# Recurrent scan of a 1024-wide block: mask tiles kept over both halves, first decays ahead of the clears, one product group moved behind another

## The chip, the cores and the metric

The kernel runs on one core of a Trainium2 chip. The metric is the device time of one execution in microseconds (us). The core has TensorE (PE: matmuls into PSUM), VectorE (DVE), ScalarE (ACT), GpSimd (POOL) and SyncE (SP), which here only issues DMAs. Each engine works through its own instructions in order and waits for the others on semaphores.

## The reference

The program is two transformer-like blocks over 512 latent and 256 context tokens, all in float32. The change touches one piece of the second block, the two-way recurrence of its even layer:

```python
def step(state, inp):
    r_t, w_t, k_t, v_t, kk_t, a_t = inp
    sa = jnp.einsum('bhvk,bhk->bhv', state, -kk_t)
    state = (state * w_t[:, :, None, :] + sa[..., None] * (kk_t * a_t)[:, :, None, :]
             + v_t[..., None] * k_t[:, :, None, :])
    return state, jnp.einsum('bhvk,bhk->bhv', state, r_t)
```

It runs forward and backward over 768 tokens, for eight heads of 64 features.

## The kernel before

The eight heads are done in two halves of four. `recurrence` runs three stages for each half: `prepare_stage` (decays, normalised keys, bonus terms), `scan_stage` (the recurrence) and `head_norm_stage`. A stage is a block of the five engines with a meeting point of all engines at its end, so nothing of a scan is issued before its preparation is over.

**The scan.** The 768 tokens are cut into 12 chunks of 64. Inside a chunk the recurrence is turned into matrix products. A 64x64 triangular inverse G is built in six levels: each level is a product group `x`, a turning `t`, a copy of both by ScalarE (`copy_xt`), a second product group `g_x`, and a masked copy into G by VectorE (`extend`). The groups of 16 small matmuls (64x64) that go with it on TensorE are:

- `a(c)`: decayed a by decayed b; `main_products(c, d)`: b and k by a and r; `b_k_turned(c)` and `v_turned(c)`: turnings;
- `z_from_chunk(c)` (L3056): the part of z that needs only the chunk (four waits: v copied, its factor masked, the state and y of the chunk before done); `z_from_state(c)`: the part that needs the state, added on top in PSUM;
- `u(c)`, `y_from_state(c)`, `s_products(c)`, `y_from_chunk(c)`: what follows from z.

Three chunks are under way at once. The order is written out by hand: a loop over q from -3 to 11 issues, on each engine, the steps of chunk q (its end), `now` = q+1 (levels 4 and 5), `new` = q+2 (levels 1 to 3) and `coming` = q+3 (its decays and first products). One turn of that loop is called a period below. Each engine's part is a list in program order, and an instruction that waits holds up all behind it on its engine.

**The start of a scan.** SP loads four constant mask tiles (`mask_before`, `masks_by_feature`, `unit_squares`, and `level_masks` as float32 into the area that the `residual` buffer lends) and, in the first half, the next keys. VectorE waits for all four, casts the level masks to 8 bits (L2935), and only then starts on the decays of chunk 0 (`decayed_a` L2868, `decayed_r` L2876). ScalarE computes the decay factors of chunk 0 (L2801), then waits for the cast before it goes on (`start_inverse` L2806, factors of chunk 1). TensorE waits for the masks and for two clears. GpSimd clears the state `S[0]` and `y` (L2775), then decays b and k of each chunk (L2784) and gathers v (L2788).

In the profile the buffers lent by `resid` are named `residual.1`, those lent by `gate_rows` (G, Z, masked a-b products, state) `gate_rows.1`, and PSUM `banks`.

Of the kernel before, what the change touches and what calls it, by code (L numbers as in the profile page):

```python
# [28 lines left out]
U8 = mybir.dt.uint8  # L29
# [332 lines left out]
def build(nc, dram, out_dram, debug=None):  # L362
# [12 lines left out]
    def sb(name, shape, dt=F32):  # L375
        return nc.alloc_sbuf_tensor(unique(name), shape, dt)

    def sem(name):
        return nc.alloc_semaphore(unique(name))
# [2116 lines left out]
    def recurrence(rcols, lora, r, k, v, mixT):  # L2496
        flat, flat2 = flat_of(resid), flat_of(gate_rows)
        with stage():
            kk = sb("kk", [P, 2, TOK])
            iclr, kdir = sb("iclr_then_b", [P, 4, TOK]), sb("k_dir", [P, 4, TOK])  # L2500
            run = sb("running_decay", [P, 4, NCH * CW])
            gam = sb("chunk_decay", [P, 2, 4, NCH])
            y = sb("y", [P, 2, TOK])
            for half in range(2):
                prepare_stage(half, rcols, lora, r, k, v, kk, iclr, kdir, run, gam, mixT, flat)
                if half == 0:
                    dump("kk", kk[:]); dump("kdir", kdir[:]); dump("run", run[:]); dump("bb", iclr[:]); dump("bv", mixT[:, 0:2, :])
                scan_stage(r, y, v, kk, iclr, kdir, run, gam, flat, flat2, k if half == 0 else None)
                head_norm_stage(half, rcols, lora, r, y, v, mixT, flat)
# [16 lines left out]

    def prepare_stage(half, rcols, lora, r, k, v, kk, iclr, kdir, run, gam, mixT, flat):

# [6 lines left out]
        with stage():  # L2535
# [10 lines left out]
            tots = sem("totals")  # L2546
            gam_made = sem("chunk_decays")
            with nc.Block() as block:
                @block.sync
                def _(sp):  # L2550
                    sp.dma_start(w2[:], dram["w2"][half]).then_inc(loaded, 16)
                    sp.dma_start(a2[:], dram["a2"][half]).then_inc(loaded, 16)
                    sp.dma_start(reset[:], dram["reset"].partition_broadcast(P)).then_inc(loaded, 16)

                @block.gpsimd
# [66 lines left out]
                def _(dve):  # L2622
# [18 lines left out]
                    dve.wait_ge(loaded, 48)  # L2641
                    scan(0)
                    scan(1)
                    finish_kdir(0)
# [29 lines left out]

    def scan_stage(r, y, v, kk, bb, kdir, run, gam, flat, flat2, k_next):


        with stage():
# [3 lines left out]
            def area(base, at, n=2):  # L2682
                return base[:, at * 256:(at + n) * 256]
# [30 lines left out]
            e = sb("decay_factors", [P, 2, 3, 4, CH])  # L2714
            before = sb("mask_before", [P, 2, CH])
            mask_H = sb("masks_by_feature", [P, 2, 4, CH])
            unit = sb("unit_squares", [P, CH])
            level = sb("level_masks", [P, LEVELS, 2, CH], U8)
            level_f32 = area(flat, 16, 3)
            loaded, zeroed, levels_cast, k_loaded = sem("loaded"), sem("zeroed"), sem("levels_cast"), sem("keys_loaded")  # L2720
            e_made, a_made, rc_made, bk_decayed = sem("factors_made"), sem("a_decayed"), sem("r_decayed"), sem("b_k_decayed")
# [40 lines left out]
            with nc.Block() as block:  # L2762
                @block.sync
                def _(sp):
                    for dst, src in ((before[:], dram["mask_before"]), (mask_H[:], dram["masks_by_feature"][:, 0:2]), (unit[:], dram["unit_squares"])):
                        sp.dma_start(dst, src).then_inc(loaded, 16)
                    sp.dma_start(level_f32, dram["level_masks"]).then_inc(loaded, 16)
                    if k_next is not None:
                        sp.dma_start(flat_of(k_next), parked_rkv[:, 2 * TOK:4 * TOK]).then_inc(k_loaded, 16)
                        sp.wait_ge(k_loaded, 16)  # L2770

                @block.gpsimd
                def _(pool):
                    for x in (S[0], y[:]):
                        nc.gpsimd.memset(x, 0.0).then_inc(zeroed, 1)  # L2775
                    for c in range(NCH):
                        if c >= 2:
                            pool.wait_ge(bkt_made, c - 1)
                        for src, places in ((bb, slice(1, 3)), (kdir, slice(0, 4, 3))):
                            for d in range(2):  # L2780
                                js = slice(2 * d, 2 * d + 2)
                                to = bk_flat[c % 2][:, d * 4 * CH:(d + 1) * 4 * CH].rearrange("p (a n) -> p a n", a=4)[:, places, :]
                                pool.wait_ge(e_made, 6 * c + 3 * d + 3)
                                nc.gpsimd.tensor_tensor(to, src[:, js, tokens(d, c)], e[:, c % 2, 2, js, :], ALU.mult).then_inc(bk_decayed, 1)  # L2784
                        if c >= 1:
                            pool.wait_ge(v_made, c)
                        for d in range(2):
                            nc.gpsimd.tensor_copy(v_now[:, d], v[:, :, tokens(d, c)]).then_inc(v_gathered, 1)  # L2788

                @block.scalar  # L2790
                def _(act):
# [40 lines left out]
                    for d in range(2):  # L2832
                        factors(0, d)
                    act.wait_ge(loaded, 64)
                    act.wait_ge(levels_cast, 1)
                    for q in range(-3, NCH):
# [24 lines left out]
                def _(dve):  # L2861
# [54 lines left out]

                    def new_state(c):
                        dve.wait_ge(s_made, c + 1)
                        nc.vector.tensor_tensor(S[(c + 1) % 2], S[c % 2], by_slot(s_out), ALU.add).then_inc(s_summed, 1)
# [5 lines left out]

                    def add_y(c):
                        dve.wait_ge(y2_made, c + 1)
                        for d in range(2):
# [4 lines left out]

                    dve.wait_ge(loaded, 64)
                    nc.vector.tensor_copy(level[:].rearrange("p l d n -> p (l d n)"), level_f32).then_inc(levels_cast, 1)  # L2935
                    dve.wait_ge(zeroed, 2)
                    dve.wait_ge(levels_cast, 1)
                    for q in range(-3, NCH):
# [32 lines left out]
                def _(pe):  # L2971
# [88 lines left out]
                    def z_from_state(c):  # L3060
                        if c >= 1:
                            pe.wait_ge(s_done, 2 * c)
# [41 lines left out]

                    pe.wait_ge(loaded, 64)
                    pe.wait_ge(zeroed, 2)
                    for q in range(-3, NCH):
# [31 lines left out]
                        if has_now:  # L3139
                            z_from_chunk(now)  # L3140
                            g_x(now, 5)
                        if has_new:
                            g_x(new, 2)
                        if coming < NCH:
                            a(coming)
# [325 lines left out]
```

## Time and profile before

| | |
|---|---|
| median of 3 runs | 3545.79 us (3544.70 to 3545.88) |
| profiled execution, own time | 3539.18 us |
| its span in the profile | 3537.4 us |
| mean granted TensorE clock | 0.948 of full |
| TensorE busy | 3202.2 us, 91% of the span |
| first scan, second scan | about 1683 to 1831 us, 1892 to 2040 us of the span |

Busy time of a matmul in the trace is pipelined and its end is modelled, so starts are read rather than ends. Line numbers (L2981) are those of the kernel before. A row of the timeline merges neighbouring instructions of one line; "x16" is their number and the length in front of the engine's name runs from the first one's start to the last one's end.

### The profile page before, as it was taken

To read this page: it belongs to the slowest core of one execution; us is meant where nothing else is said; L and a number is where in the kernel's file an instruction comes from. 1 tells how busy PE (TensorE), PEld (TensorE's weight loads), DVE (VectorE), ACT (ScalarE), POOL (GpSimd) and SP (SyncE) were. 2 spreads that over 40 slices of the span, in tenths; PEclk is the share of its full clock that TensorE was granted. 3 is DMA by queue.
4 is the path that set the end of the run, shared out by engine and by line. 5 is a ranking of instruction groups with operands and counts; after the bars stand their busy time and mean duration, and the time that the engine had idled before them with its cause. 6 is when DMAs were issued, how large, how long until landed. Compare 5 with 4: busy or idle time off the path is not lost. (4 is left out here: it accounts for less than half of the span.)

```text
span 3537.4 us, 53773 instructions
## 1 busy us (share of the span) xinstructions
PE 3202.2 (91%) x21886; PEld 2573.6 (73%) x21886; DVE 2208.1 (62%) x3940; ACT 1298.0 (37%) x2245; POOL 146.5 (4%) x222
## 2 busy tenths in 40 slices
PE   6989999997899969987887989998999998889999
PEld 5768877655788758865665867887887876678777
DVE  7678866696788675667555637554666336653344
ACT  2343333324433333245534534222233335642243
POOL 0300000200000000000211100000000000000000
PEclk9989999999999989998898989999999999999999
DMA  7424553112233422120000022333232121022221
GB/s 303 168 101 179 190 179 113 61 36 66 97 140 135 143 102 85 60 89 12 20 33 11 4 85 108 119 119 108 107 143 107 54 98 59 1 78 96 81 104 60
DMA packets 64773, 340.78 MB, mean 96 GB/s; under 512 B 15120, under 2 KB 16656, under 8 KB 29072
## 3 DMA queue, kind: packets, MB, share of 16 engines
q1 hardware_dynamic: 61616, 325.51, 26.2%
q0 software_dynamic: 2048, 9.48, 0.8%
q8 instruction: 174, 2.85, 0.3%
q10 hardware_dynamic: 864, 2.36, 0.2%
q14 instruction: 71, 0.58, 0.1%
HBM read 326.53 MB, written 10.79 MB: 95 GB/s over the span
## 5 line engine op out<-in xcount | busy, mean ns | idle before, releaser
L265 DVE TENSOR_TENSOR weight_lo<-weight_ring,weight_hi 128x1024 fp32r<-128x1024 f32 x341 | 423.1, 1242 | 170.2 <-ACT weight_hi L250 165.1
L250 ACT CAST weight_hi<-weight_ring 128x1024 fp32r<-128x1024 f32 x341 | 356.0, 1044 | 158.0 <-PE banks L422 91.9
L420 PE MATMUL banks<-hT_hi.1,weight_hi 128*128 128x512 f32 x896 | 365.7, 408 | 25.5 <-PEq L383 23.5
L421 PE MATMUL banks<-hT_lo.1,weight_hi 128*128 128x512 f32 x896 | 358.8, 400 | 0.0
L422 PE MATMUL banks<-hT_hi.1,weight_lo 128*128 128x512 f32 x896 | 358.5, 400 | 0.0
L420 PEld LDWEIGHTS banks<-hT_hi.1,weight_hi 128*128 128x128 f32 x896 | 171.4, 191 | 68.7 <-issue 26.4
L422 PEld LDWEIGHTS banks<-hT_hi.1,weight_lo 128*128 128x128 f32 x896 | 171.1, 191 | 41.9
L421 PEld LDWEIGHTS banks<-hT_lo.1,weight_hi 128*128 128x128 f32 x896 | 171.3, 191 | 41.5 <-issue 1.9
L420 PE MATMUL banks<-hT_hi.3,weight_hi 128*128 128x512 f32 (+1 forms) x512 | 174.6, 341 | 0.0
L422 PE MATMUL banks<-hT_hi.3,weight_lo 128*128 128x512 f32 (+1 forms) x512 | 173.3, 338 | 0.0
L421 PE MATMUL banks<-hT_lo.3,weight_hi 128*128 128x512 f32 (+1 forms) x512 | 173.1, 338 | 0.0
L319 DVE SCALAR_TENSOR_TENSOR side_sum<-weight_ring,silu_c2.1,side_sum 128x256 f32<-128x256 f32 x336 | 160.4, 477 | 0.1
L319 DVE SCALAR_TENSOR_TENSOR weight_ring<-weight_ring,silu_c2.1 128x256 f32<-128x256 f32 x336 | 160.3, 477 | 0.0
L531 PE MATMUL banks<-weight_hi,left_hi.6 128*128 128x512 f32 x360 | 145.8, 405 | 9.3 <-DVE weight_lo L265 9.3
L534 PE MATMUL banks<-weight_lo,left_hi.6 128*128 128x512 f32 x360 | 142.8, 397 | 0.0
L533 PE MATMUL banks<-weight_hi,left_lo.6 128*128 128x512 f32 x360 | 142.1, 395 | 0.0
L319 DVE SCALAR_TENSOR_TENSOR weight_ring<-weight_ring,silu_c1.1 128x256 f32<-128x256 f32 x280 | 135.6, 484 | 10.5
L420 PE MATMUL banks<-hT_hi.2,weight_hi 128*128 128x256 f32 (+1 forms) x336 | 115.1, 343 | 2.7 <-PEq L383 2.7
L421 PE MATMUL banks<-hT_lo.2,weight_hi 128*128 128x256 f32 (+1 forms) x336 | 114.1, 340 | 0.0
L422 PE MATMUL banks<-hT_hi.2,weight_lo 128*128 128x256 f32 (+1 forms) x336 | 114.0, 339 | 0.0
L422 PEld LDWEIGHTS banks<-hT_hi.3,weight_lo 128*128 128x128 f32 x512 | 96.4, 188 | 11.6
L421 PEld LDWEIGHTS banks<-hT_lo.3,weight_hi 128*128 128x128 f32 x512 | 96.6, 189 | 11.0
(746 smaller groups left out, 7324.1 us busy)
## 6 DMA issues: line engine op xcount, KB each, us to landing
weight_ring<-ff SPq DMA_DIRECT2D x64, 1024.0 KB, 5.0
weight_ring<-ada SPq DMA_DIRECT2D x48, 1024.0 KB, 4.8
weight_ring<-up SPq DMA_DIRECT2D x44, 1024.0 KB, 6.9
weight_ring<-ada_ffn SPq DMA_DIRECT2D x24, 1024.0 KB, 4.9
weight_ring<-down SPq DMA_DIRECT2D x20, 1024.0 KB, 4.9
weight_ring<-ada_mix SPq DMA_DIRECT2D x16, 1024.0 KB, 4.8
first_blocks.1<-ada_mix SPq DMA_DIRECT2D x8, 1024.0 KB, 11.9
weight_ring<-cv_in SPq DMA_DIRECT2D x8, 1024.0 KB, 4.8
```

What stands on the lines that cost most here:

```text
L250: self.nc.scalar.copy(hi, raw).then_inc(self.hi_made, 1)
L265: self.nc.vector.tensor_tensor(lo, raw, hi.bitcast(F32), ALU.subtract).then_inc(self.lo_made, 1)
L319: ins = self.nc.vector.scalar_tensor_tensor(out=to, in0=w[:, k, :], scalar=vec[:, k, v:v + 1], in1=to, op0=ALU.mult, op1=ALU.add)
L420: nc.tensor.matmul(out, w_hi, x_hi, start=first, stop=False)
L421: nc.tensor.matmul(out, w_hi, x_lo, start=False, stop=False)
L422: return nc.tensor.matmul(out, w_lo, x_hi, start=False, stop=last)
L531: one = nc.tensor.matmul(out, xh, hi[:, kk, :], start=(k == 0), stop=False)
L533: nc.tensor.matmul(out, xl, hi[:, kk, :], start=False, stop=False)
L534: last = nc.tensor.matmul(out, xh, lo[:, kk, :], start=False, stop=(k == k_tiles - 1))
```

## The change

Four edits:

1. The four mask tiles are allocated once for both halves. `prepare_stage` of half 0 loads them behind its own three loads on SP's queue, and VectorE casts the level masks between its first two scans over tokens. The scans load no masks and wait for none.
2. On GpSimd, the first chunk's decays of b and k come ahead of the clear of the state, and the clear of `y` comes behind the second chunk's.
3. The waits for the two clears move to the first instructions that need them.
4. On TensorE, `z_from_chunk(now)` moves from ahead of `g_x(now, 5)` to behind `g_x(new, 2)`.

```diff
+            masks = (sb("mask_before", [P, 2, CH]), sb("masks_by_feature", [P, 2, 4, CH]), sb("unit_squares", [P, CH]),
+                     sb("level_masks", [P, LEVELS, 2, CH], U8))
 ...
+            masks_loaded, levels_cast = sem("masks_loaded"), sem("levels_cast")
+            level_f32 = flat[:, 16 * 4 * CH:16 * 4 * CH + LEVELS * 2 * CH]
 ...
                     sp.dma_start(reset[:], dram["reset"].partition_broadcast(P)).then_inc(loaded, 16)
+                    if masks is not None:
+                        before, by_feature, unit, _ = masks
+                        sp.dma_start(level_f32, dram["level_masks"]).then_inc(masks_loaded, 16)
+                        sp.dma_start(before[:], dram["mask_before"]).then_inc(masks_loaded, 16)
+                        sp.dma_start(by_feature[:], dram["masks_by_feature"][:, 0:2]).then_inc(masks_loaded, 16)
+                        sp.dma_start(unit[:], dram["unit_squares"]).then_inc(masks_loaded, 16)
+                        sp.wait_ge(masks_loaded, 64)
 ...
                     scan(0)
+                    if masks is not None:
+                        dve.wait_ge(masks_loaded, 64)
+                        nc.vector.tensor_copy(masks[3][:].rearrange("p l d n -> p (l d n)"), level_f32).then_inc(levels_cast, 1)
                     scan(1)
 ... (scan_stage, SP)
-                    for dst, src in ((before[:], dram["mask_before"]), (mask_H[:], dram["masks_by_feature"][:, 0:2]), (unit[:], dram["unit_squares"])):
-                        sp.dma_start(dst, src).then_inc(loaded, 16)
-                    sp.dma_start(level_f32, dram["level_masks"]).then_inc(loaded, 16)
 ... (scan_stage, GpSimd)
-                    for x in (S[0], y[:]):
-                        nc.gpsimd.memset(x, 0.0).then_inc(zeroed, 1)
-                    for c in range(NCH):
+                    decay_bk(0)
+                    nc.gpsimd.memset(S[0], 0.0).then_inc(zeroed, 1)
+                    gather_v(0)
+                    decay_bk(1)
+                    nc.gpsimd.memset(y[:], 0.0).then_inc(zeroed, 1)
+                    gather_v(1)
+                    for c in range(2, NCH):
+                        decay_bk(c)
+                        gather_v(c)
 ... (scan_stage, ScalarE)
-                    act.wait_ge(loaded, 64)
-                    act.wait_ge(levels_cast, 1)
 ... (scan_stage, VectorE; new_state(0) now waits for zeroed 1, add_y(0) for zeroed 2)
-                    dve.wait_ge(loaded, 64)
-                    nc.vector.tensor_copy(level[:].rearrange("p l d n -> p (l d n)"), level_f32).then_inc(levels_cast, 1)
-                    dve.wait_ge(zeroed, 2)
-                    dve.wait_ge(levels_cast, 1)
 ... (scan_stage, TensorE; z_from_state(0) now waits for zeroed 1)
-                    pe.wait_ge(loaded, 64)
-                    pe.wait_ge(zeroed, 2)
 ...
                         if has_now:
-                            z_from_chunk(now)
                             g_x(now, 5)
                         if has_new:
                             g_x(new, 2)
+                        if has_now:
+                            z_from_chunk(now)
                         if coming < NCH:
                             a(coming)
```

## Rows read from the trace of the kernel before

**Rows 1.** The page's first line.

```profile
span 3537.4 us, 53773 instructions
```

**Rows 2.** Stretches: length, busy time by engine, clock granted, DMA share, GB/s.

```profile
1683.00:1689.70 6.70, 0.00 (x0) 0.00 (x0) 1.26 (x5) 2.02 (x9) 3.75 (x8) 0.50 0.65 201
...
1700.00:1702.00 2.00, 1.86 (x50) 1.44 (x44) 0.96 (x3) 1.49 (x5) 1.35 (x5) 0.89 0.00 0
...
1720.80:1731.50 10.70, 10.28 (x304) 8.81 (x304) 7.03 (x21) 6.09 (x18) 2.24 (x6) 1.00 0.02 5
1908.00:1909.00 1.00, 0.99 (x33) 0.80 (x32) 0.17 (x1) 0.95 (x3) 0.81 (x3) 0.68 0.00 0
```

**Rows 3.** Timeline, start of both scans: start, length, instruction, idle before and releaser.

```profile
1683.26 1.31 ACT L2801 ACTIVATE decay_factors.1<-running_decay.1 128x128 f32<-128x128 f32 x6 [15.51 <-PEq L383]
...
1685.66 0.86 POOL L2784 TENSOR_TENSOR residual.1<-k_dir.1,decay_factors.1 128x128 f32<-128x128 f32 x2
...
1688.33 0.56 DVE L2935 CAST level_masks.1<-residual.1 128x768 uint8<-128x768 f32 x1 [6.11 <-DMA residual.1<-level_masks]
1688.99 0.49 DVE L2868 SCALAR_TENSOR_TENSOR residual.1<-kk.1,decay_factors.1 128x128 f32<-128x128 f32 x2
...
1689.30 1.31 ACT L2801 ACTIVATE decay_factors.1<-running_decay.1 128x128 f32<-128x128 f32 x6
...
1689.74 0.70 PE L2981 MATMUL banks<-residual.1 64*64 64x64 f32 x16 [15.49 <-DVE residual.1 L2868]
1690.08 1.06 POOL L2784 TENSOR_TENSOR residual.1<-iclr_then_b.1,decay_factors.1 128x128 f32<-128x128 f32 x2 [3.09 <-ACT decay_factors.1 L2801]
1690.38 2.08 PE L2999 MATMUL banks<-residual.1 64*128 64x128 f32 x16
1691.09 0.87 POOL L2784 TENSOR_TENSOR residual.1<-k_dir.1,decay_factors.1 128x128 f32<-128x128 f32 x2
...
1898.36 0.71 PE L2981 MATMUL banks<-residual.1 64*64 64x64 f32 x16 [15.69 <-DVE residual.1 L2868]
```

**Rows 4.** One line's instructions, ns min/median/max of one: the decays on GpSimd and VectorE.

```profile
L2784 POOL TENSOR_TENSOR residual.1<-iclr_then_b.1,decay_factors.1 x24: 453/460/464, 1684.8 to 1796.9; 128x128 f32<-128x128 f32 x24
L2868 DVE SCALAR_TENSOR_TENSOR residual.1<-kk.1,decay_factors.1 x24: 271/274/291, 1689.0 to 1801.7; 128x128 f32<-128x128 f32 x24
```

**Rows 5.** Waits of the first scan, 1710 to 1830 us: total, times, longest.

```profile
PE banks L2981 <- DVE gate_rows.1 L2889: 4.3, 10, 0.4
...
PE banks L3056 <- DVE gate_rows.1 L2924: 1.0, 1, 1.0
...
PE banks L3027 <- DVE gate_rows.1 L2889: 0.7, 1, 0.7
```

**Rows 6.** Timeline of a middle period, around the moved group.

```profile
1729.56 1.07 ACT L2810 COPY x_t.1<-banks 128x512 f32<-128x512 f32 x2 [1.25 <-PE banks L3033]
...
1730.33 0.62 PE L3056 MATMUL banks<-residual.1 64*64 64x64 f32 x13
...
1730.73 0.27 PE L3042 MATMUL banks<-x_t.1 64*64 64x64 f32 x1
...
1731.32 0.78 DVE L2889 COPY_PREDICATED gate_rows.1<-level_masks.1,banks 128x256 f32<-128x256 uint8 x2 [1.08 <-PE banks L3042]
...
1731.91 0.46 PE L2981 MATMUL banks<-residual.1 64*64 64x64 f32 x16 [0.43 <-DVE gate_rows.1 L2889]
...
1732.17 0.44 PE L3027 MATMUL banks<-gate_rows.1 64*64 64x64 f32 x16
```

**Rows 7.** Timeline of the first preparation.

```profile
1644.24 0.42 SPq L2553 DMA_DIRECT2D reset.1<-reset  x1
...
1650.35 2.91 PE L2571 MATMUL banks<-lora.1,w2.1 128*128 128x512 f32 x4
...
1658.36 1.78 DVE L2627 TENSOR_TENSOR_SCAN running_decay.1<-reset.1,residual.1 128x780 f32<-128x780 f32 x1 [1.61 <-ACT residual.1 L2609]
```

**Rows 8.** DMA issues from 1643 to 1700 us: KB each, us to landing.

```profile
reset.1<-reset SPq DMA_DIRECT2D x1, 390.0 KB, 4.7
```

More of the change, by code:

```diff
@@ L2503, in recurrence @@
             y = sb("y", [P, 2, TOK])
+            masks = (sb("mask_before", [P, 2, CH]), sb("masks_by_feature", [P, 2, 4, CH]), sb("unit_squares", [P, CH]),
+                     sb("level_masks", [P, LEVELS, 2, CH], U8))
             for half in range(2):
-                prepare_stage(half, rcols, lora, r, k, v, kk, iclr, kdir, run, gam, mixT, flat)
+                prepare_stage(half, rcols, lora, r, k, v, kk, iclr, kdir, run, gam, mixT, flat, masks if half == 0 else None)
                 if half == 0:
                     dump("kk", kk[:]); dump("kdir", kdir[:]); dump("run", run[:]); dump("bb", iclr[:]); dump("bv", mixT[:, 0:2, :])
-                scan_stage(r, y, v, kk, iclr, kdir, run, gam, flat, flat2, k if half == 0 else None)
+                scan_stage(r, y, v, kk, iclr, kdir, run, gam, flat, flat2, masks, k if half == 0 else None)
                 head_norm_stage(half, rcols, lora, r, y, v, mixT, flat)
@@ L2525, in spread_to_features, with prepare_stage @@
         return last
-    def prepare_stage(half, rcols, lora, r, k, v, kk, iclr, kdir, run, gam, mixT, flat):
+    def prepare_stage(half, rcols, lora, r, k, v, kk, iclr, kdir, run, gam, mixT, flat, masks):
         f0 = 2 * half
@@ L2671, in _, with scan_stage @@
                             step(nc.vector.tensor_tensor(mixT[:, f0 + f, seg], ps[4 + 2 * f + s][:, 0:seg.stop - seg.start], v[:, f, seg], ALU.mult))
-    def scan_stage(r, y, v, kk, bb, kdir, run, gam, flat, flat2, k_next):
+    def scan_stage(r, y, v, kk, bb, kdir, run, gam, flat, flat2, masks, k_next):
         with stage():
@@ L2714, in scan_stage @@
             e = sb("decay_factors", [P, 2, 3, 4, CH])
[L2715 to L2720, printed above, removed]
+            before, mask_H, unit, level = masks
+            zeroed, k_loaded = sem("zeroed"), sem("keys_loaded")
             e_made, a_made, rc_made, bk_decayed = sem("factors_made"), sem("a_decayed"), sem("r_decayed"), sem("b_k_decayed")
@@ L2773, in _, with decay_bk @@
                 def _(pool):
-                    for x in (S[0], y[:]):
-                        nc.gpsimd.memset(x, 0.0).then_inc(zeroed, 1)
-                    for c in range(NCH):
+                    def decay_bk(c):
                         if c >= 2:
@@ L2784, in _, with gather_v @@
                                 nc.gpsimd.tensor_tensor(to, src[:, js, tokens(d, c)], e[:, c % 2, 2, js, :], ALU.mult).then_inc(bk_decayed, 1)
+                    def gather_v(c):
                         if c >= 1:
@@ L2917, in new_state @@
                     def new_state(c):
+                        if c == 0:
+                            dve.wait_ge(zeroed, 1)
                         dve.wait_ge(s_made, c + 1)
@@ L2926, in add_y @@
                     def add_y(c):
+                        if c == 0:
+                            dve.wait_ge(zeroed, 2)
                         dve.wait_ge(y2_made, c + 1)
@@ L3060, in z_from_state @@
                     def z_from_state(c):
-                        if c >= 1:
+                        if c == 0:
+                            pe.wait_ge(zeroed, 1)
+                        else:
                             pe.wait_ge(s_done, 2 * c)
```

## The prediction

> **What bounds the kernel now.** I read the page for the size of the whole [rows 1], then only the two scans, since all the rest of the program is untouched except for four loads and one cast. Each scan has two different limits. At its start TensorE does nothing and runs at the low clock: in the 6.70 us from 1683.00 it has no matmul and a granted clock of 0.50, while ScalarE has 2.02 us of work and GpSimd 3.75 [rows 2]. The timeline says who ends that wait: VectorE sat 6.11 us until the level masks had landed, cast them in 0.56 us, and decayed a at 1688.99; TensorE's first product came at 1689.74, and at 1898.36 in the second scan, the same pattern 208.6 us later [rows 3]. In the middle of a scan TensorE is the limit: busy 10.28 us of a period of 10.70, at full clock [rows 2]. The idle time left is one gap per period, ahead of `a(coming)`, ended by VectorE's masked copy: 4.3 us over 10 periods, 0.43 each [rows 5].
>
> **Start of a scan: masks and decays (edits 1 to 3).** Without the load nothing holds VectorE or TensorE but the decays themselves. Their own pace stands in the same trace, for chunk 1: ScalarE's six factors start at 1689.30, GpSimd's decays of b end at 1690.08 + 1.06 = 1691.14, those of k at 1691.09 + 0.87 = 1691.96 [rows 3], so 1.84 and 2.66 us behind the factors' start. The factors of chunk 0 start at 1683.26 already [rows 3]. With the decays first on GpSimd, b is ready at 1683.26 + 1.84 = 1685.10 and k at 1685.92. From the end of the last decay to the first product is 1689.74 - 1689.48 = 0.26 (VectorE's two took 1688.99 + 0.49). So `a(0)` starts near 1685.35 and `main_products(0)`, which needs k, near 1686.15, against 1689.74 and 1690.38 [rows 3]: 4.4 and 4.2 earlier, and everything behind follows the second. VectorE's share (four factors of about 0.2, then 0.27) is done near 1684.5 and isn't last. I take 4.2 us per scan.
>
> Of this, 3.6 come from the masks: with the clears still ahead, k would be ready at 1685.66 + 0.86 = 1686.52, 0.6 later [rows 3]. What is late next is GpSimd's second decay of k; behind it now stand the clear of the state, the gather of v, chunk 1's decays (four of 0.46 [rows 4]), done near 1688.6, and the clear of y. Chunk 1's are wanted by `a(1)`, which before came 10 us behind `a(0)`; the clears are wanted by the first state and y, later still. All of that is covered.
>
> GpSimd's decays will now run beside VectorE's, which before they did only in part. The decays show no sign of each other over the scan: 453 to 464 ns on GpSimd, 271 to 291 on VectorE [rows 4]. I add nothing; the upper bound is VectorE's two decays put end to end with GpSimd's, 0.55 us per scan. The Trainium skill (GPSIMD Engine Reference, Specifications) says that GpSimd shares its SBUF interface with VectorE and contends with VectorE instructions that have two SBUF inputs, which these have; by that rule the start would gain 3.7 instead of 4.2, and the trace so far speaks against it.
>
> **First preparation.** SP issues four more loads, about 736 KB, behind `reset` (issued at 1644.24, landed 4.7 us later, near 1648.9) [rows 7, 8]. TensorE needs that one at 1650.35, 1.4 us later [rows 7]. The four follow at some 0.5 us each and, at the same 4.7 us to landing, are in by about 1652, and VectorE reaches the cast near 1656.7, with 1.61 us idle until 1658.36 [rows 7] for a cast of 0.56 [rows 3]. Both cost nothing. If the new loads slow `reset` down, the worst is their whole time at the 201 GB/s seen [rows 2], 3.7 us, less the cover of 1.4: 2.3 us, once. I take 0. The second preparation gets nothing new, and what SP issued at a scan's start only goes away; the load of the next keys starts earlier and nobody waits for it.
>
> **The moved group (edit 4).** In the middle period `z_from_chunk` starts at 1730.33 and the two `g_x` groups follow from 1730.73 on, VectorE extends at 1731.32, `a(coming)` starts at 1731.91 and `x(new, 3)` at 1732.17 [rows 6]. `z_from_chunk` holds the queue for 0.40 ahead of work that VectorE waits for, and 0.43 of idle time follows: the group can lie in the gap. It is bounded by ScalarE: its two copies start at 1729.56 and take 1.07 for both [rows 6], so level 5's is done near 1730.14 and level 2's at 1730.63. `g_x(now, 5)` can thus start at 1730.33, `g_x(new, 2)` at about 1730.78 and end its issue at 1731.17, `z_from_chunk` runs to 1731.57, and `a(coming)` starts there, 0.34 earlier. VectorE starts its first copy 0.40 earlier, near 1730.92, its second near 1731.30, done at 1731.74; 0.12 on, `x(new, 3)` starts at 1731.86: 0.31 earlier. Everything behind is TensorE's own queue. So 0.31 us per period, from 0.15 (if the extra group delays `a` and the copies come late) to the whole gap, 0.43. The group's four waits no longer stand ahead of the `g_x` pair but ahead of `a` and `x(new, 3)`; all four are met before the group's old place in a middle period.
>
> There are 10 such gaps, and two turns without `coming`: 0.7 idle ahead of `x(11, 3)`, where I take 0.4, and 1.0 ahead of the last `z_from_chunk`, which there waits for the state [rows 5], with `g_x(11, 5)` queued behind it. The last `g_x` now fills that wait, worth 0.3. Per scan 10 x 0.31 + 0.4 + 0.3 = 3.8.
>
> **The clock.** It rose at 1700.4 (0.89 over 2.00 us is 0.44 us at the low level) and at 1908.6 (0.68 over 1.00 is 0.64) [rows 2], so 10.7 and 10.3 us behind the first product [rows 3]. At 0.50 it is the 1.2 GHz level, and it is there before the scan starts, so a shorter idle time doesn't spare it. The 16 products of `a` took 0.70 at the low level and 0.46 at the full one [rows 3, 6]. If the rise comes 4 us later against the work, these 4 us of mostly TensorE work cost 4 x (1 - 0.46/0.70) = 1.4; if 4 us earlier, they give that back. I take 0.5 loss per scan, since the start is made denser only at its head. The Trainium skill (TensorE: Matmul & The Clock Gate, What's actually happening) says that the number of slow matmuls differs between executions of one kernel; two scans here differ by 0.4 us.
>
> **Sum.** 2 x 4.2 + 2 x 3.8 - 2 x 0.5 = 15.0 us. The span of 3537.4 becomes 3522.4 and the profiled execution's own 3539.2 becomes 3524.2. That execution was 6.6 us under the median of the runs; taken from the median 3545.8, the time is 3530.8, 0.42% less.
>
> **The rivals.**
>
> - *The moved group gives nothing:* ScalarE's copies of x and t hold `g_x(now, 5)` where it was, and `z_from_chunk` takes the gap without moving `a`. For it: the second copy ends only 0.1 ahead of the pair's old start. Against: the first one is 0.2 early. Time: 3545.8 - 8.4 + 1.0 = 3538.4, just over 0.2% faster. Chance 0.1.
> - *The clock takes back the start:* the rise comes 4 us later against the work in both scans: 3545.8 - 16.0 + 2.8 = 3532.6. Chance 0.2, in the range.
> - *Both of these together*, or a start that gains only half because a decay is late: 3545.8 - 8.4 + 2.8 = 3540.2, no difference that can be told. Chance 0.06.
> - *Slower:* the clock stays at 1.2 GHz for whole periods, because the first products now come in a thinner stream after the idle start. A period then takes 10.28 x 0.70/0.46 + 0.4 = 16.0, 5.3 more. Against 16 us gained it needs 16/5.3, some 3 periods in all, to reach equality, and 4.3, over two in each scan, to be 7 us slower: 3553. Both scans rose within the first 11 us here. Chance 0.02.
> - *The chain as summed:* 0.62.
>
> **How the numbers follow.** 0.2% is 7.1 us, about what a measurement of this kernel tells from no change. The low end of the range is the whole gap in every period (22 x 0.12 = 2.6 more) and a clock that costs nothing (1.0) with a little of an earlier rise: 3526. The high end takes in the later clock, the slowed `reset` and most of the first rival: 3538. Faster 0.92, same 0.06, slower 0.02.
>
> **What will show it.** In the trace after: no mask load and no cast between the preparation and the first product of a scan; `a(0)` some 2.2 us behind the first factors instead of 6.5; `main_products(0)` released by GpSimd; the gap ahead of `a(coming)` under 0.15 and the period 10.4 instead of 10.7; a first preparation of the same length; the clock's rise 10 to 14 us behind the first product. The prediction fails if the period stays at 10.7 (a second limit of equal length, on VectorE or ScalarE), if the first product comes later than 1686, or if the clock rises periods later.

## The result, and the profile after

| | time, us |
|---|---|
| before, median of 4 runs | 3545.25 (3544.70 to 3545.88) |
| changed, median of 4 runs | 3523.03 (3520.29 to 3526.26) |
| ratio, 95% interval | 0.9938 (0.992 to 0.9955) |
| profiled execution of the changed kernel | 3520.44, span 3518.7 |
| forecast | 3530.8, range 3526 to 3538 |

The kernel became 22 us faster (16 to 28 by the interval); 15 were forecast, and 3523.0 lies 3 us under the range. Execution against execution, the profiled one of before took 3539.2 and the profiled one after 3520.4: 18.8 less. Over this whole study, 19 runs of the changed kernel have a median of 3523.7, 19.8 us under the 3543.5 of 48 runs of before beside them. One more run of before took 3737.4 us with a mean granted clock of 0.82, a slower state that some executions have, and is left out.

The start of a scan in the timeline of the changed kernel, the answer to [rows 3]. The lines of its code are shifted: the factors are L2818, the decays L2883 and L2789, the first products L2996, the main products L3014.

```profile
1682.05 1.31 ACT L2818 ACTIVATE decay_factors.1<-running_decay.1 128x128 f32<-128x128 f32 x6 [15.54 <-PEq L383]
...
1682.39 0.29 DVE L2883 SCALAR_TENSOR_TENSOR residual.1<-kk.1,decay_factors.1 128x128 f32<-128x128 f32 x1 [1.41 <-ACT decay_factors.1 L2818]
1682.99 0.45 DVE L2883 SCALAR_TENSOR_TENSOR residual.1<-kk.1,decay_factors.1 128x128 f32<-128x128 f32 x1 [0.31 <-ACT decay_factors.1 L2818]
1683.36 0.74 DVE L2891 TENSOR_TENSOR residual.1<-r.1,decay_factors.1 128x128 f32<-128x128 f32 x2
...
1682.83 1.12 POOL L2789 TENSOR_TENSOR residual.1<-iclr_then_b.1,decay_factors.1 128x128 f32<-128x128 f32 x2 [38.79 <-ACT decay_factors.1 L2818]
1683.92 0.92 POOL L2789 TENSOR_TENSOR residual.1<-k_dir.1,decay_factors.1 128x128 f32<-128x128 f32 x2
...
1684.10 0.71 PE L2996 MATMUL banks<-residual.1 64*64 64x64 f32 x16 [10.09 <-POOL residual.1 L2789]
1684.98 2.08 PE L3014 MATMUL banks<-residual.1 64*128 64x128 f32 x16 [0.18 <-POOL residual.1 L2789]
```

The mask load and the cast are gone, and TensorE is released by GpSimd. From the first factors to the first product it is now 2.05 us instead of 6.48, to the main products 2.93 instead of 7.12: 4.4 and 4.2 earlier, as summed.

The middle of a period, the answer to [rows 6]: `g_x` is L3057, the moved group L3071, the masked copies L2904.

```profile
1712.93 1.07 ACT L2827 COPY x_t.1<-banks 128x512 f32<-128x512 f32 x2 [1.25 <-PE banks L3048]
...
1713.70 0.82 PE L3057 MATMUL banks<-x_t.1 64*64 64x64 f32 x32
1714.35 0.68 PE L3071 MATMUL banks<-residual.1,masked_ak.1 64*64 64x64 f32 x16
1714.83 0.46 PE L2996 MATMUL banks<-residual.1 64*64 64x64 f32 x16
1715.11 0.44 PE L3042 MATMUL banks<-gate_rows.1 64*64 64x64 f32 x16
...
1714.23 0.81 DVE L2904 COPY_PREDICATED gate_rows.1<-level_masks.1,banks 128x256 f32<-128x256 uint8 x2 [0.54 <-PE banks L3057]
```

Stretches of one period each, and of one us around the clock's rise, the answer to [rows 2] (length, busy PE, PEld, DVE, ACT, POOL, granted clock, DMA share, GB/s):

```profile
1703.41:1713.70 10.29, 10.29 (x305) 8.89 (x305) 7.07 (x20) 6.20 (x18) 2.24 (x6) 1.00 0.02 5
1713.70:1724.00 10.30, 10.30 (x309) 8.91 (x308) 7.07 (x20) 6.22 (x18) 2.23 (x6) 1.00 0.01 3
...
1694.00:1695.00 1.00, 1.00 (x33) 0.86 (x32) 0.19 (x1) 0.95 (x4) 0.82 (x3) 0.62 0.00 0
...
1896.00:1897.00 1.00, 1.00 (x20) 0.76 (x22) 0.43 (x2) 0.45 (x3) 0.57 (x2) 0.92 0.00 0
```

Both `g_x` groups start right behind the turnings, the moved group lies under VectorE's copies, and the wait ahead of the next chunk's first products, 4.3 us in ten before [rows 5], is gone. TensorE is shown busy for the whole period of 10.3 us, which was 10.7. (A busy TensorE is not yet one that sets the pace: the runs with half of the z group, below, tell what does.)

The first preparation, the answer to [rows 7]:

```profile
1643.05 0.42 SPq L2557 DMA_DIRECT2D reset.1<-reset  x1
1643.51 0.86 SPq L2560 DMA_DIRECT2D residual.1<-level_masks  x1
...
1649.43 2.91 PE L2582 MATMUL banks<-lora.1,w2.1 128*128 128x512 f32 x4
...
1655.74 0.54 DVE L2656 CAST level_masks.1<-residual.1 128x768 uint8<-128x768 f32 x1
1657.11 1.78 DVE L2638 TENSOR_TENSOR_SCAN running_decay.1<-reset.1,residual.1 128x780 f32<-128x780 f32 x1 [0.83 <-ACT residual.1 L2620]
```

The cast lies in VectorE's idle time, of which 0.83 us is left. The four loads did delay `reset`: it landed 5.5 us after its issue instead of 4.7, near 1648.6, still 0.9 ahead of TensorE's product at 1649.43. From the preparation's first load to the scan's first factors it took 39.86 us, and 39.87 before.

The length of a scan is read from the first factors to the first load of the stage behind it (g2). For before, whose scan starts at 1683.26 [rows 3], and for the changed kernel, whose first starts at 1682.05 above:

```profile
1831.94 0.33 SPq L3174 DMA_DIRECT2D g2.1<-g  x1
...
1891.87 1.31 ACT L2801 ACTIVATE decay_factors.2<-running_decay.1 128x128 f32<-128x128 f32 x6 [15.51 <-PEq L383]
...
2040.57 0.33 SPq L3174 DMA_DIRECT2D g2.2<-g  x1
```

```profile
1821.76 0.33 SPq L3190 DMA_DIRECT2D g2.1<-g  x1
...
1882.69 1.31 ACT L2818 ACTIVATE decay_factors.2<-running_decay.1 128x128 f32<-128x128 f32 x6 [15.53 <-PEq L383]
...
2022.56 0.33 SPq L3190 DMA_DIRECT2D g2.2<-g  x1
```

That is 148.7 us in both scans before (the second from 1891.87 to 2040.57) and 139.7 and 139.9 after: 8.9 per scan, 17.8 in both, where the prediction had 8.0 and took 0.5 off for the clock. The rest of the 18.8 us between the two executions, 1.0, lies outside the scans: that part of the span took 3240.0 us before and 3239.1 after.

### The profile page after: what moved, and what is told of

It reads as the page before. It is cut to its first block and busy times, and to the rows that moved or that the text cites. A ratio compares the mean times of both kernels' runs of the same rounds, so it can differ in the third digit from the quotient of the medians.

```text
span 3518.7 us, 53769 instructions
## 1 busy us (share of the span) xinstructions
PE 3202.9 (91%) x21886; PEld 2573.2 (73%) x21886; DVE 2209.3 (63%) x3939; ACT 1297.6 (37%) x2245; POOL 146.6 (4%) x222
## 5 line engine op out<-in xcount | busy, mean ns | idle before, releaser
L319 DVE SCALAR_TENSOR_TENSOR weight_ring<-weight_ring,silu_c1.1 128x256 f32<-128x256 f32 x280 | 135.6, 484 | 10.5
L422 PEld LDWEIGHTS banks<-hT_hi.3,weight_lo 128*128 128x128 f32 x512 | 96.4, 188 | 11.7
L420 PEld LDWEIGHTS banks<-hT_hi.3,weight_hi 128*128 128x128 f32 x512 | 96.5, 189 | 11.0
```

What stands on the lines that cost most here:

```text
L319: ins = self.nc.vector.scalar_tensor_tensor(out=to, in0=w[:, k, :], scalar=vec[:, k, v:v + 1], in1=to, op0=ALU.mult, op1=ALU.add)
L420: nc.tensor.matmul(out, w_hi, x_hi, start=first, stop=False)
L422: return nc.tensor.matmul(out, w_lo, x_hi, start=False, stop=last)
```

## The experiments

All times are in us; "scans" are the two scans of the profiled execution, measured as above, and "rise" is the time from a scan's first product to the rise of the granted clock, in each of the two. The profiled execution is one of the runs, and not always near their median: those of the z group only (3533.5) and of the warm tail (3527.6) are among the slowest of theirs.

| run | median (runs) | before, run beside it | ratio (95%) | scans | rise |
|---|---|---|---|---|---|
| changed kernel, first profile (above) | 3523.0 (4) | 3545.3 | 0.9938 (0.992 to 0.9955) | 139.7, 139.9 | 10.7, 11.4 |
| changed kernel, again | 3524.3 (5) | 3544.2 | 0.9942 (0.993 to 0.9955) | 143.3, 139.7 | 23.3, 11.2 |
| masks only | 3534.9 (10) | 3544.2 | 0.9974 (0.9965 to 0.9983) | 148.9, 148.8 | 23.8, 23.6 |
| masks and order | 3530.2 (5) | 3544.2 | 0.996 (0.9947 to 0.9972) | 144.6, 144.7 | 10.6, 11.2 |
| z group only | 3529.1 (5) | 3544.2 | 0.996 (0.9946 to 0.9973) | 147.7, 148.5 | 23.1, 23.7 |
| half of the z group, old place | 3537.6 (1) | 3542.5 | not measured | 146.5, 149.7 | 10.5, 23.2 |
| half of the z group, new place | 3529.0 (1) | 3542.5 | not measured | 139.4, 144.2 | 11.6, 23.6 |
| warm tail | 3518.4 (6) | 3542.5 | 0.9934 (0.992 to 0.9949) | 139.9, 143.4 | 11.9, 23.4 |
| warm tail and head | 3522.4 (5) | 3542.5 | 0.9944 (0.993 to 0.9958) | 139.7, 140.1 | 11.4, 11.7 |
| fill | 3517.4 (6) | 3542.6 | 0.9928 (0.9914 to 0.9942) | 136.8, 136.7 | high from the start |
| changed kernel, third | 3521.3 (5) | 3542.6 | 0.994 (0.9927 to 0.9952) | 144.5, 139.5 | 23.8, 10.9 |
| fill, again | 3512.8 (5) | 3542.1 | 0.9915 (0.9901 to 0.9929) | 137.8, 136.8 | high from the start |
| changed kernel, fourth | 3523.7 (5) | 3542.1 | 0.9949 (0.9936 to 0.9962) | 139.9, 143.8 | 11.8, 23.9 |

**The changed kernel again.** No edit.

> The changed kernel once more, unaltered. Theory A (the change itself is worth about 17 to 19 us, and the rest of the 22.2 us between the two medians is a step of 5 to 6 us in the untouched part that single executions take or don't take): single times fall on two levels, near 3520 and near 3526, and the runs of before on two levels too, near 3539 and 3545; compared level by level the gain is 18.5 to 19.5 us. Theory B (the gain is 22 us everywhere, the profile of before at 3539.2 was a stray): all runs of before stand at 3544.5 to 3546 and those of this kernel centre on 3523.

Single times were 3518.0, 3520.2, 3524.3, 3525.3 and 3528.3, and those of before spread from 3539.8 to 3548.7. That is a spread of 9 to 10 us in both, without the two levels of theory A. Theory B's narrow group of before falls: 3539.2 was no stray. On the size of the gain the run doesn't decide: 19.8 between the medians, 16 to 25 by the interval, allows both A's 17 to 19 and B's 22. A part of the spread lies outside the scans: the rest of the program took between 3235.2 and 3243.6 us in the fourteen profiles of this study, though only the first preparation (edit 1) and the filling products of some runs touch it. Another part lies inside the scan. Stretches of its first scan, whose first product is at 1683.81:

```profile
1681.75:1693.75 12.00, 7.36 (x93) 5.81 (x93) 4.92 (x13) 5.24 (x20) 5.57 (x12) 0.50 0.20 67
1693.75:1705.75 12.00, 10.97 (x190) 9.10 (x190) 4.81 (x13) 4.83 (x15) 2.23 (x6) 0.50 0.00 1
...
1707.00:1709.00 2.00, 2.00 (x84) 1.68 (x76) 1.38 (x4) 1.28 (x5) 1.36 (x5) 0.98 0.00 0
```

The clock stood at its low level (0.50, so 1.2 GHz) through both stretches of 12 us and rose at 1707.1, 23.3 us behind the first product. In the first profile of the same code it rose after 10.7 and 11.4. This scan took 143.3 us, the other one of the same execution 139.7: a late rise costs 3.5. In the later profiles of the changed kernel the scan with the late rise was 4.9 (144.5) and 3.9 (143.8) longer than the other; in the one of 144.5 the clock also fell for 3.4 us from 1818.8 on, 6 us ahead of the scan's end. Of the changed kernel's eight profiled scans three rose late. What makes a rise late stays open.

**The masks alone.** The changed kernel with this on GpSimd and the z group in its old place (the waits for the clears stay where edit 3 put them, which decides nothing here, since GpSimd clears ahead of its decays again):

```diff
-                    decay_bk(0)
-                    nc.gpsimd.memset(S[0], 0.0).then_inc(zeroed, 1)
-                    gather_v(0)
...
+                    for x in (S[0], y[:]):
+                        nc.gpsimd.memset(x, 0.0).then_inc(zeroed, 1)
+                    for c in range(NCH):
```

> Edit 1 alone: mask tiles kept and loaded in the first preparation; the clears still ahead of the decays on GpSimd and the z group in its old place. My working gave 3.6 us per scan for it, so 7.2 us in all, and the start of the first main products near 3.5 us behind the first factors (4.2 less 0.6). Rival: the start is worth more than summed, because the clock rises earlier against the work: 9 us or more. Periods stay at 10.7 to 10.8 us in both.

Its timeline, with the first factors at 1679.90:

```profile
1682.50 0.70 PE L2992 MATMUL banks<-residual.1 64*64 64x64 f32 x16 [10.63 <-POOL residual.1 L2789]
1683.32 2.08 PE L3010 MATMUL banks<-residual.1 64*128 64x128 f32 x16
```

Main products 3.42 us behind the factors, 3.7 earlier than before; 3.6 were summed. The median is 9.2 us under before (6 to 12 by the interval), which allows the 7.2 summed and the rival's 9. The profile's scan lengths alone would have misled: both scans had a late rise and took 148.9 and 148.8 us, as long as before's with an early one. The start had come 3.7 us earlier and a rise 13 us later had taken it back.

**Masks and order.** The changed kernel with only the z group back in its old place, ahead of `g_x(now, 5)` instead of behind `g_x(new, 2)`:

```diff
-                            z_from_chunk(now)
...
+                            z_from_chunk(now)
```

> The changed kernel with the z group back in its old place: edits 1 to 3. By my sum 8.4 us faster than before, 4.2 per scan, with main products 2.9 us behind the first factors and periods of 10.7 to 10.8 us. Rival (GpSimd and VectorE held each other up at the start, and the new order gives nothing over the masks alone): 7.2 us, like edit 1 alone.

With the first factors at 1678.26, and the wait ahead of `a(coming)` in the middle of its scan:

```profile
1680.31 0.71 PE L2996 MATMUL banks<-residual.1 64*64 64x64 f32 x16 [10.09 <-POOL residual.1 L2789]
1681.20 2.08 PE L3014 MATMUL banks<-residual.1 64*128 64x128 f32 x16 [0.18 <-POOL residual.1 L2789]
```

```profile
PE banks L2996 <- DVE gate_rows.1 L2904: 4.3, 10, 0.4
```

Both rises were early here, so the scans compare with before: 144.6 and 144.7 against 148.7, so 4.1 and 4.0 per scan, where 4.2 were summed. The median is 13.9 us under before (10 to 19 by the interval), above the 8.4 expected; what the medians have beyond the scans stays open. Main products come 2.94 us behind the factors, 0.48 sooner than with the masks alone (0.6 summed), so the order on GpSimd does count, and the rival falls. The gap of 0.43 per period is still there.

**The z group alone.** The kernel before with the one move of the last edit.

> The kernel before with only the z group moved behind the second g_x. My prediction put 0.31 us on each period and 3.8 on a scan, 7.6 us in all. What the trace after suggests instead: the whole gap, 0.43 us per period and 5.0 per scan, 10 us in all. Rival (the moved group pays only once the masks are gone): under 4 us. The start of the scans stays as it was.

From one `a(coming)` to the next in the middle of its first scan:

```profile
1711.83 0.46 PE L2981 MATMUL banks<-residual.1 64*64 64x64 f32 x16
...
1722.09 0.46 PE L2981 MATMUL banks<-residual.1 64*64 64x64 f32 x16
```

10.26 us, and 10.28 in most turns, where before has 10.72: the whole gap is closed, with the masks in their old place too, so the two edits don't need each other. The median fell 15 us, more than the 10 expected, with an interval of 10 to 19. The two profiled scans seem to say the reverse, 147.7 and 148.5, but their clock rose only 23.1 and 23.7 us behind the first product. The medians of this run and the one above add up to 29 us, against 19.8 for the whole change beside them: the intervals of medians of five reach 4 to 5 us to either side here, and the parts are better read from the traces.

**Half of the z group, in both places.** Both kernels, with the products of direction 1 left out, so that their y is not the reference's (one execution each):

```diff
-                        for d in range(2):
+                        for d in range(1):
                             for h in range(2):
                                 for f in range(2):
                                     s = slot(h, 2 * d + f)
```

> The kernel before with half of the z group's products left out (only direction 0 of z_from_chunk, so y is not the reference's). If the group in its old place stands on the path of every period, as the prediction has it, halving it takes 0.20 us off each period: 10.5 instead of 10.7. If the gap ahead of the next chunk's first products absorbs it, the period stays at 10.7.

> The changed kernel with the same half of the z group left out. If the group now lies in the time in which VectorE extends the inverse, halving it takes nothing off the period: 10.3 stays, with a gap of 0.1 to 0.2 us ahead of the next group. If TensorE's own queue is now the only limit, the period falls by the 0.20 us left out, to 10.1.

Two periods of each, first with the group in its old place:

```profile
1712.17:1722.66 10.49, 10.05 (x297) 8.59 (x297) 7.04 (x21) 6.19 (x18) 2.23 (x6) 1.00 0.02 5
1722.66:1733.14 10.48, 10.05 (x296) 8.58 (x297) 7.04 (x21) 6.19 (x18) 2.23 (x6) 1.00 0.01 4
```

```profile
1709.50:1719.78 10.28, 10.26 (x296) 8.76 (x297) 7.08 (x21) 6.19 (x18) 2.23 (x6) 1.00 0.01 3
1719.78:1730.06 10.28, 10.26 (x297) 8.76 (x297) 7.07 (x21) 6.20 (x18) 2.24 (x6) 1.00 0.02 6
```

And VectorE's first copy and `a(coming)` with half of the group in its new place:

```profile
1708.91 0.81 DVE L2904 COPY_PREDICATED gate_rows.1<-level_masks.1,banks 128x256 f32<-128x256 uint8 x2 [2.05 <-PE banks L3057]
...
1709.50 0.46 PE L2996 MATMUL banks<-residual.1 64*64 64x64 f32 x16
```

In its old place half of the group is worth 0.22 to 0.24 us of a period (10.48 against 10.70), and the gap behind it stays. In its new place it is worth nothing: 10.28 against 10.29. So the path ran through the group before and no longer does. What it runs through now is VectorE's pair of masked copies: `a(coming)` starts 0.59 to 0.60 us behind the start of the first one in the kernel before (1731.32 to 1731.91), in the changed one (1714.23 to 1714.83) and with half of the group (1708.91 to 1709.50). The busy time doesn't show it, since it stays at 10.26 of 10.28 us with the half left out.

**Warming TensorE ahead of a scan.** Two kernels that try to bring the rise forward. The first adds five products to the idle tail of each preparation; the second has two more at the head of the scan (below the dots):

```diff
+                    pe.wait_ge(kk_scaled, 1)
+                    for _ in range(5):
+                        nc.tensor.matmul(ps[0], head_ones[:], lora[:, 0, 0:BANK], start=True, stop=True)
...
+                    for _ in range(2):
+                        nc.tensor.matmul(ps[7][:, 0:256], ident[:], flat_of(v)[:, 0:256], start=True, stop=True)
```

> The changed kernel plus five products of 128x512 on TensorE in the idle tail of each preparation, written to a PSUM bank that nobody reads again; nothing waits for them. So far the clock rose 10 to 11 us behind a scan's first product in some scans and 23 to 24 us behind it in others, and the late rise made one scan 3.5 us longer. Theory A (the idle stretch before a scan sets the low clock, and work in it brings the rise forward): no scan rises later than 10 us behind its first product, scans last 136 to 139.8 us instead of 139.8 or 143.3, and the median falls 4 to 9 us below the changed kernel's 3524. Theory B (the rise is not moved by work placed there): the same two lengths of scan, and a median within 2 us of 3524.

> The same, with two more products of 128x256 at the very head of each scan's TensorE list, ahead of the first real product, while GpSimd still decays. If theory A holds and the gap of about 3 us between the tail and the first product matters, this is faster than the tail alone by up to 3 us; at the low clock the two cost some 1.7 us, which end before the first product could start, so it is not slower by more than 1 us. If B holds, the same as the changed kernel or up to 1 us slower.

The second scan of the first one, whose last filling product ends at 1882.26 and whose first real product starts at 1887.37:

```profile
1883.00:1885.00 2.00, 0.00 (x0) 0.00 (x0) 1.17 (x3) 0.00 (x0) 0.00 (x0) 1.00 0.00 0
...
1886.00:1887.00 1.00, 0.00 (x0) 0.00 (x0) 0.75 (x3) 1.00 (x6) 0.77 (x2) 0.91 0.05 16
1887.00:1888.00 1.00, 0.63 (x16) 0.55 (x16) 0.37 (x1) 1.00 (x6) 1.00 (x3) 0.50 0.00 0
...
1910.00:1912.00 2.00, 2.00 (x77) 1.67 (x79) 0.95 (x3) 1.85 (x6) 0.97 (x4) 0.82 0.00 0
```

The clock was high in the tail, fell at 1886.83 after 4.6 us without work (from 1882.26), half a us ahead of the first real product, and rose again at 1910.7, 23.3 us behind it. In its first scan it fell sooner, at 1685.4, 2.8 us behind the last filling product. The second kernel left 3.1 us between its two stretches of filling, and the clock fell there too (at 1678.8 and 1880.2, 2.8 and 3.1 us behind the last product of the tail). Both have the scans of theory B, 139.7 to 140.1 and one of 143.4; the lower median of the first isn't clear of noise against the changed kernel's.

**Filling without a gap.** Seven products in the tail, four at the head, and small ones in the first turns: two each behind the first `t`, behind the first `g_x` and behind the first main products (below, in the order of the code):

```diff
+                    pe.wait_ge(kk_scaled, 1)
+                    for _ in range(7):
+                        nc.tensor.matmul(ps[0], head_ones[:], lora[:, 0, 0:BANK], start=True, stop=True)
...
+                    def fill(n, width):
+                        for _ in range(n):
+                            nc.tensor.matmul(ps[7][:, 0:width], ident[:], flat_of(v)[:, 0:width], start=True, stop=True)
+
+                    fill(4, 256)
...
+                        if q == -2:
+                            fill(2, 128)
...
+                        if q == -2:
+                            fill(2, 128)
...
+                        if q == -3:
+                            fill(2, 256)
```

> The changed kernel with TensorE kept at work from the tail of each preparation into the first turns of the scan: seven products of 128x512 in the tail, four of 128x256 at the scan's head, two of 128x256 behind the first main products, and two of 128x128 each behind the first t and the first g_x. In the two runs with less filling the clock was at its high level in the tail and fell 4 to 5 us behind the last filling product. Theory A (the clock holds as long as TensorE is never idle for some us): it stays high through the first turns, scans last 136 to 138 us, the median falls to 3514 to 3519, and no late rises. Theory B (the thin stream of small products in the first turns lowers it whatever stands before): it falls within the first turns and rises 10 to 25 us behind the first product as before; the filling then costs up to 2 us per scan at the low level and the median is 3522 to 3528.

> The changed kernel once more on this chip, for comparison with the run above. Median 3520 to 3526; each scan 139.8 us, or 143.3 where the clock rises late; 18 to 21 us faster than before.

Its first scan starts at 1681.56. Two stretches around its head, and its first products in the timeline:

```profile
1681.00:1683.00 2.00, 1.42 (x7) 1.29 (x8) 0.79 (x3) 1.44 (x7) 0.51 (x2) 1.00 0.37 49
1683.00:1685.00 2.00, 1.51 (x27) 1.02 (x27) 1.06 (x3) 1.38 (x7) 2.00 (x6) 1.00 0.79 326
```

```profile
1683.62 0.46 PE L2999 MATMUL banks<-residual.1 64*64 64x64 f32 x16
1684.50 1.16 PE L3017 MATMUL banks<-residual.1 64*128 64x128 f32 x16 [0.42 <-POOL residual.1 L2792]
```

The clock stays at 1.00 from the tail to the last us of the scan, the first group takes 0.46 instead of 0.71 and the main products 1.16 instead of 2.08, and the scans take 136.8 and 136.7 us, 3.0 less than the changed kernel's 139.7 and 139.9 with early rises. The longest time without a product between tail and scan is 1.4 us. Theory A holds for this filling. It differs from the one before it in three places at once (two more products in the tail, two more at the head, the small ones in the turns), and no run tells which of them was needed. The median was 3517.4, 3.9 under the changed kernel's beside it, which by itself isn't clear of noise.

> The filling version once more, to see whether its lead over the changed kernel holds: scans of 136.7 us both with the clock high from their first product on, against 139.8 (or 143 to 144.5 with a late rise); a median 5 to 9 us under the changed kernel's in this same session. If the clock does fall in some executions after all, a scan of 140 us or more shows it and the lead is under 3 us.

> The changed kernel beside it in the same session: median 3520 to 3526, 18 to 21 us under before.

3512.8 (3509.7 to 3513.5) against 3523.7 (3522.2 to 3524.8) and 3542.1: 11 us under the changed kernel, more than expected, and 29 under before. Scans of 137.8 and 136.8; the changed kernel beside it had 139.9 and, with a late rise, 143.8. The 137.8 is a scan in which the clock did fall, not at its start but for 3.4 us from 1814.0 on, 6 us ahead of its end. In these runs the filling version beats both.

## Why the prediction was right or wrong

**Start of a scan: right, and by some luck so close.** 4.2 us were summed; the trace shows 4.2 at the main products, and the run with edits 1 to 3 has scans 4.0 to 4.1 shorter. The split into masks (3.6 summed, 3.7 seen) and order (0.6 summed, 0.5 seen) holds. Chunk 1's pace could nearly stand for chunk 0's: k's decays were done 2.79 us behind the factors (1683.92 + 0.92) where 2.66 were summed, and the main products followed 0.14 behind their end where 0.26 was taken. The two errors of 0.12 to 0.13 cancel.

**GpSimd beside VectorE: wrong that they don't disturb each other, though it costs next to nothing here.** One line's instructions after, ns min/median/max, the answer to [rows 4]:

```profile
L2789 POOL TENSOR_TENSOR residual.1<-iclr_then_b.1,decay_factors.1 x24: 453/458/522, 1682.8 to 1788.1; 128x128 f32<-128x128 f32 x24
...
L2883 DVE SCALAR_TENSOR_TENSOR residual.1<-kk.1,decay_factors.1 x24: 273/277/451, 1682.4 to 1792.4; 128x128 f32<-128x128 f32 x24
...
L2891 DVE TENSOR_TENSOR residual.1<-r.1,decay_factors.1 x24: 277/282/543, 1683.4 to 1797.3; 128x128 f32<-128x128 f32 x24
```

The longest of VectorE's decays of a went from 291 to 451 ns (1682.99), the longest of r from 293 to 543 (1683.56), and GpSimd's from 464 to 522 (1683.43): all three at the scan's start, where they now run side by side. In the rest of the scan the decays kept their length. The rule of the Trainium skill (GPSIMD Engine Reference, Specifications) was set aside because the old trace showed no such thing; it did not, since there these decays hardly met. This trace agrees with the rule. VectorE's loss of 0.2 to 0.3 us doesn't reach the path, since it sits idle for 0.76 us behind it; GpSimd's, some 0.1, is in the 2.79 above. By the rule the prediction made the start's gain 3.7, and that is not what came: the upper bound of 0.55 was not reached.

**First preparation: right**, 39.86 us against 39.87. The loads took 0.8 us of the 1.4 us of cover that `reset` had.

**The moved group: right in kind, too small in size.** "So 0.31 us per period" was the step that failed; it is 0.43 (10.29 to 10.30 against 10.70 to 10.72), the whole gap, which stood as the upper end. My working moved VectorE's first copy by no more than the 0.40 for which the group had held the queue, and added 0.12 between the end of VectorE's copies and TensorE's next group, where the rows that it used show 0.07 (1731.32 + 0.78 to 1732.17). The turn's `x`, before and after:

```profile
1728.46 0.69 PE L3027 MATMUL banks<-gate_rows.1 64*64 64x64 f32 x32
```

```profile
1711.83 0.69 PE L3042 MATMUL banks<-gate_rows.1 64*64 64x64 f32 x32
```

In the trace after, the pair of `g_x` starts 0.77 us behind ScalarE's copies, as summed, and runs unbroken, so VectorE's copies start 2.40 us behind that turn's `x` (1711.83 to 1714.23), which was 2.86 before (1728.46 to 1731.32): 0.46 gained where 0.40 was summed. The next group again follows 0.07 behind their end. Per scan the group is worth 4.8 us (144.6 to 139.8) where 3.8 were summed: 4.3 in the ten gaps instead of 3.1, and so about 0.5 in the two last turns instead of 0.7.

**The clock: the wrong treatment.** Taking 0.5 us per scan off for it has no support: with an early rise there is nothing to take off (10.7 and 11.4 us after, 10.7 and 10.3 before). And its range was wrong. I priced a rise 4 us later at 1.4 us, since two scans of one execution agreed within 0.4. Rises 23 to 24 us behind the first product occur in the same code, 12 to 13 us later than the early ones, and cost 3.5 to 3.9 us a scan, 4.9 where the clock fell once more near the end. The price per us was nearly right (12.5 us at 0.34 gives 4.3); how much later a rise can come was not. So the second rival, the clock taking back the start, is what some executions do, and it moves single times and medians by several us in either direction.

**The sum.** 15.0 forecast, plus 2.0 for the moved group, plus 1.0 not lost to the clock, gives 18.0; the scans of the two first profiles differ by 17.8, and these executions by 18.8. The two mis-sized terms are 3.0 of the 7.8 us by which the forecast of 3530.8 was too high. With them right it would have been 3527.8, still over the measured 3523.0. Of the other 4.8 us, 2.3 lie in where it started from (3545.8, against 3543.5 for the 48 runs of before) and 0.7 in the four runs of the result (3523.0, against 3523.7 for all 19). That leaves 1.8 us between the 19.8 of all medians and the 18.0 of the terms, and its cause stays open. All intervals of the changed kernel allow 17.8. A possible part is that the profiled execution of before had two early rises and its timed runs, 4 to 6 us slower, mostly not; only one profile of before exists, so this is argued and not shown. The forecast was taken from the median by way of that profile, and the range gave no room for a term that both kernels carry and that differs from run to run: single times of one kernel spread over 9 to 10 us, the part outside the scans alone over 8.

## What to carry to other kernels

When an engine that bounds a loop has one gap per turn, look for a group ahead of the gap that nobody in the gap's chain needs, and move it in. Here that gave the whole gap, 0.43 us per turn, with a group that had held the queue for about as long, 0.40, and 0.20 with half of that group (10.48 to 10.28). Both fit a gain of the smaller of the group's length and the gap; a group longer than the gap was not run. Price a freed start by how the same steps run for the next chunk, where they no longer wait. Where a stage starts after an idle time of TensorE, compare several profiles before a part of the change is judged by one: here the clock's rise alone hid 4 us per stage, and products that nobody needs, put into the idle time so that no long gap was left, took another 3 us off each scan.

## What the runs showed of the hardware

- In the two runs with less filling the granted clock fell to its low level 2.8 to 4.6 us behind the last filling product of a preparation, with 128x512 products back to back ahead of that; in the two where the longest gap there was 1.4 us it stayed at 1.00 through the thin stream of small groups at the scan's start.
- After the start of a scan it rose 10.3 to 11.9 us behind the first product in some scans and 23.1 to 23.9 in others, for the same code, and a late rise made a scan of the changed kernel 3.5 to 3.9 us longer, 4.9 with another fall of 3.4 us near its end.
- VectorE's 128x128 operations with two SBUF inputs took up to 451 and 543 ns beside GpSimd's, against a median of 277 and 282; GpSimd's took up to 522 beside them, against 458.
